# Two FFN tiles computed together, row block by row block, at the start of each FFN

## What is computed

```python
def swiglu(h, w1, w3, w2):
    return (jax.nn.silu(h @ w1) * (h @ w3)) @ w2
...
        yp = yp + swiglu(rmsnorm(yp, norm_ffn_g[l]), ffn_w1[l], ffn_w3[l], ffn_w2[l])
        ys = ys + swiglu(rmsnorm(ys, norm_ffn_g[l]), ffn_w1[l], ffn_w3[l], ffn_w2[l])
```

## Time and profile before

| | |
|---|---|
| time, median of 3 runs | 2050.66 us (2047.96 to 2051.35) |
| the profiled execution | 2048.34 us, span 2046.6 us |
| TensorE matmul (PE) busy | 1942.4 us, 95% |
| VectorE (DVE) busy | 742.4 us, 36% |
| ScalarE (ACT) busy | 450.3 us, 22% |
| mean granted TensorE clock | 0.965 of full |
| matmuls on `h_split` | 5184, 768.6 us busy |

### The profile page before, as it was taken

The page is one execution under the profiler, slowest core; times in us unless marked ns, Lnnn a source line. Parts: engine busy times, 40 slices in busy tenths (PEclk is TensorE's granted clock), DMA queues, the critical chain, the costliest instruction groups (busy, mean ns, idle before and its releaser), DMA issues.

```text
span 2046.6 us, 26656 instructions
## 1 busy us (share of the span) xinstructions
PE 1942.4 (95%) x11462; PEld 1622.3 (79%) x11462; DVE 742.4 (36%) x1203; ACT 450.3 (22%) x714; POOL 141.5 (7%) x149
## 2 busy tenths in 40 slices
PE   7999989899889999999998999799988999999998
PEld 5755556655659999999996999565565999999998
DVE  2099843312444332233334131631245333223222
ACT  3200231101422211111222114430133211121111
POOL 3001000000000000000004332200000000000000
PEclk9999986699999999999999999899999999999999
DMA  6322130150021112312120343411402211221120
GB/s 226 124 70 66 43 124 2 45 205 30 13 103 59 65 57 77 103 61 69 57 93 18 103 64 81 157 67 52 185 11 103 82 55 57 97 89 61 63 90 32
DMA packets 32036, 161.71 MB, mean 79 GB/s; under 512 B 8584, under 2 KB 9224, under 8 KB 18016
## 3 DMA queue, kind: packets, MB, share of 16 engines
q1 hardware_dynamic: 24032, 122.16, 18.1%
q0 software_dynamic: 7936, 38.60, 5.1%
HBM read 150.07 MB, written 10.42 MB: 78 GB/s over the span
## 4 chain that ended last, share of the span: by engine, by line
PE 92%; DVE 4%; ACT 2%; issue 1%; DMA 0%; POOL 0%; ACTq 0%; DVEq 0%
PE G L614 84%; PE Q L614 4%; PE S L614 3%; ACT rstd L1099 1%; DVE front L1417 1%; PE Q L1032 1%; DVE work L1721 1%; DVE h_split L1725 1%; ACT work L1099 0%; PE Q L884 0%; DVE stats L1836 0%; DMA front<-in_mem 0%; DVE front L1849 0%; DVE front L1619 0%; DVE stats L1659 0%
## 5 line engine op out<-in xcount | busy, mean ns | idle before, releaser
L614 PE MATMUL G<-h_split,w_split 128*128 128x320 f32 x5184 | 768.6, 310 | 10.6 <-DVE h_split L1725 10.5
L614 PEld LDWEIGHTS G<-h_split,w_split 128*128 128x128 f32 x5184 | 764.4, 189 | 12.8 <-issue 8.9
L614 PE MATMUL G<-front,ring 128*128 128x512 f32 (+2 forms) x1792 | 486.9, 434 | 12.4 <-DVE front L1417 7.0
L614 PEld LDWEIGHTS G<-front,ring 128*128 128x128 f32 x1792 | 279.5, 193 | 218.9 <-issue 212.6
L614 PE MATMUL G<-g_split,w_split 128*128 128x320 f32 x2112 | 310.4, 309 | 0.0
L614 PEld LDWEIGHTS G<-g_split,w_split 128*128 128x128 f32 x2112 | 309.9, 188 | 0.0
L1453 DVE TENSOR_TENSOR w_split<-ring,w_split 128x1024 fp32r<-128x1024 f32 (+2 forms) x152 | 164.4, 1083 | 359.3 <-ACT w_split L1099 359.3
L1099 ACT ACTIVATE w_split<-ring 128x1024 fp32r<-128x1024 f32 (+2 forms) x172 | 164.4, 957 | 517.8 <-PE G L614 517.8
L1503 DVE SCALAR_TENSOR_TENSOR front<-front,par 128x512 f32<-128x512 f32 x240 | 111.6, 546 | 0.1
L1099 ACT ACTIVATE work<-G 128x640 f32<-128x640 f32 x52 | 36.7, 706 | 331.9 <-PE G L614 331.9
L1737 DVE TENSOR_TENSOR work<-work,G 128x640 f32<-128x640 f32 x44 | 36.1, 821 | 183.9 <-PE G L614 183.9
(11 more groups left out here) (211 smaller groups left out, 1118.1 us busy)
## 6 DMA issues: line engine op xcount, KB each, us to landing
ring<-in_w_up0a SPq DMA_DIRECT2D x11, 1024.0 KB, 4.8
ring<-in_w_up0b SPq DMA_DIRECT2D x11, 1024.0 KB, 4.8
ring<-in_w_up1a SPq DMA_DIRECT2D x11, 1024.0 KB, 4.7
ring<-in_w_up1b SPq DMA_DIRECT2D x11, 1024.0 KB, 4.8
front<-in_mem_k POOLq DMA_DIRECT2D x8, 1024.0 KB, 11.7
front<-in_mem_v POOLq DMA_DIRECT2D x8, 1024.0 KB, 14.4
ring<-in_w_down0a SPq DMA_DIRECT2D x8, 704.0 KB, 4.1
ring<-in_w_down0b SPq DMA_DIRECT2D x8, 704.0 KB, 4.1
```

Source lines behind the costliest of these rows:

```text
L614: return nc.tensor.matmul(out, lhsT, rhs, start=start, stop=stop, **kw)
```

## The change

A new function `split_pair` computes tiles n and n + 1 together. For each row block k it waits once for the activations' low part, issues the 6 matmuls of tile n, and then the 6 of tile n + 1. The FFN's half "a" uses it for its first two tiles; half "b" and the loops are as before. Only TensorE's instructions are touched.

```diff
+            def split_pair(n, p, rhs, normed):
+
+
+                for j in range(2):
+                    begin(n + j)
+                pe.wait_ge(split, p + 2)
+                for k in range(KD):
+                    pe.wait_ge(applied, normed + k)
+                    for j in range(2):
+                        for wpart, xpart in ((0, 0), (0, 1), (1, 0)):
+                            w = ws[:, j, wpart, k * P:(k + 1) * P]
+                            for f in range(2):
+                                fr = slice(f * HT, (f + 1) * HT)
+                                m = mm(GF[(n + j) % 2][:, fr], w, rhs[:, xpart, k, fr],
+                                       k == 0 and wpart + xpart == 0, k == KD - 1 and wpart == 1)
+                        if k == KD - 1:
+                            m.then_inc(tile_done, 1)
+
...
-                    first = APPLIED[f"ffn{l}"] - KD + 1 if half == "a" else None
-                    for j in range(2):
-                        split_product(t0 + j, j, p0 + j, KD, hs, normed=first if j == 0 else None)
+                    if half == "a":
+                        split_pair(t0, p0, hs, APPLIED[f"ffn{l}"] - KD + 1)
+                    else:
+                        for j in range(2):
+                            split_product(t0 + j, j, p0 + j, KD, hs)
```

## The result

The changed kernel takes 2052.95 us (median of 20 runs, 2049.18 to 2055.51); the kernel before takes 2049.36 us (median of 20 runs, 2044.80 to 2051.35). The ratio is 1.0017, with a 95% interval from 1.0011 to 1.0023: slower by some 3.5 us, under the 0.2% that the prediction set as its bound. The prediction was 2053.0 us, with a range from 2049 to 2056.

A forecast was written before the change was run, and what follows sets the result against it. TensorE, busy 95% of the span, was taken as the bound. Row waits -3.9 and stalls +4.8 made +0.9 us; with one 1.5 us clock drop, +2.4 on the median 2050.66, stated as 2053.0 us, range 2049.0 to 2056.0.

The forecast's parts named there:

- all three sums: Whole kernel: +0.9 us with no clock drop behind the stalls, +2.4 with one, +3.9 with both.
- The end of the row waits: First two tiles of each FFN: all row waits but the first go, gaining 1.6 and 2.3 us, together 3.9.
- 3.5 us at half speed do 13: Second FFN's start: half speed lasts 3.5 us and covers 13 matmuls; the other 83 take 12.2 us.
- the two prices: TensorE's time per matmul: 0.147 us at full speed, about 0.267 us at half speed.
- The stall: Before each FFN's third tile: TensorE idles 2.3 us for split weights; 2.4 us per FFN with restart cost, 4.8 in all.
- the slow first matmul: Third tile's start, after the wait: 0.1 us added to each 2.3 us stall, as an estimate.
- The clock's price: Behind each stall: a half-speed stretch of 3.4 us costs 1.5 us, with two chances in three per stall.
- What lay behind it: Work queued after the stall: delay is taken once, fourth tile's weights are in time, loop stays at 7.04 us a tile.
- One sign was worded wrongly: Sign in the changed profile: ScalarE's first two reads of the FFN's tiles come 0.9 us apart in place of 7.04.
- The bank rule: Rival, first two tiles: alternating PSUM banks keeps all 96 matmuls at half speed; +20 us, 2071 us; chance 0.02.
- The stall stays small: Rival, before the third tile: the hidden chain is off the path, 3.9 us are kept, 2046.8 us; chance 0.06.
- The longer stretch of 6.8 us: Rival, third tile: half speed lasts 6.8 us, each stall costs 2.4 + 3.1 us; +7.1, 2057.8 us; chance 0.11.

The follow-up runs named there:

- the lag of five: Changed kernel with tile B five row blocks behind tile A (36 matmuls of B follow A's last): ratio 0.9975, again 0.9975 in the second run.
- the kernel with extra matmuls: Changed kernel with 14 extra matmuls, read by nobody, between the pair of tiles and the third tile: ratio 1.0002 against the kernel before.
- The lags: Changed kernel with tile B 1, 2, 3 or 5 row blocks behind tile A (changed kernel itself is 0): first ratios 0.9993, 0.9996, 0.9982, 0.9975.
- early weights and table: Changed kernel with the third tile's weights split early into a free buffer part and the SiLU table loaded ahead by a one-column SiLU: ratio 0.9986.
- the lag of three: Changed kernel with tile B three row blocks behind tile A (24 matmuls of B follow A's last): ratio 0.9982, then 0.9985 in the second run.
- the lag of one: Changed kernel with tile B one row block behind tile A (12 matmuls of B follow A's last): ratio 0.9993.
- the lag of two: Changed kernel with tile B two row blocks behind tile A (18 matmuls of B follow A's last): ratio 0.9996, then 0.9993 in the second run.
- the second experiment: Changed kernel with the third tile's weights split early into a free buffer part and each loop's first group written out, no early table load: ratio 0.9995.

## Why the prediction was right

**What was luck.** The prediction of 2053.0 us is 2.4 us on a base of 2050.66, the median of 3 runs. Measured were 3.6 us on a base of 2049.36, the median of 20. The two differences, 1.2 and 1.3 us, cancel, and so 2052.95 came out. The range held all three sums, with no half-speed stretch, one or two, so the time alone bears out none of them; the traces do.

**The end of the row waits.** Right in kind and size for the first FFN: the gate tile was read at 627.18, and the predicted end of the pair puts that at 627.85 - 0.88 + 0.2 = 627.17, so 1.6 us were gained. For the second FFN 2.3 us were predicted and 1.7 came. The term "3.5 us at half speed do 13" did not hold there: in the changed kernel the half level lasted to 1575.6 from a start at 1570.82, 4.8 us:

```profile
1570.80:1575.50 4.70, 4.68 (x18) 4.70 (x19) 4.70 (x7) 2.21 (x3) 0.00 (x0) 0.50 0.02 3
...
1575.00:1576.00 1.00, 1.00 (x7) 1.00 (x6) 1.00 (x3) 0.30 (x1) 0.00 (x0) 0.68 0.00 0
```

I had taken the length of that stretch from the one execution as if it belonged to the place. It is 3.0 to 6.1 us in the starts compared here (the shortest in the second FFN with the lag of five, the longest in that of the kernel with extra matmuls). Each microsecond of it takes some 0.45 us from the gain, worked out from the two prices: 1 - 0.147 / 0.267.

**The stall.** Predicted 2.3 us, or 2.4 with the slow first matmul; the trace shows 2.12 us of idling after the modelled end of the last matmul, and the third tile began at 630.14, where the sum gives 627.85 + 2.3 = 630.15. The lags are the proof that it is this chain: 2.12, 1.24, 0.36 us and nothing, with 6, 12, 18 and 24 matmuls to cover it, and nothing with early weights and table.

**The clock's price.** 1.5 us a stretch was predicted, and 1.52 measured with the extra matmuls. Wrong was the choice among the three sums: I took one drop as the middle (+2.4), and both stalls were followed by half speed, in both executions. With both, the prediction had +3.9; the FFN's starts of the trace give +4.5 (0.6 from the second FFN's smaller gain), and the runs +3.5, with an interval from 2.3 to 4.7.

**What lay behind it.** The product of gate and up tile and the next low part were in time, as predicted, and the loop kept 7.04 us a tile. One sign was worded wrongly: it is VectorE that reads the up tile, not ScalarE. What stood close together were ScalarE's two roundings of weights (from 627.78, 1.99 us for both), the second of which waits for the up tile.

**The bank rule.** The 96 matmuls over four PSUM banks ran as the sum at 0.267 and 0.147 us each says, in one stretch of 16.61 us, and with the cover restored nothing is lost. The Trainium skill's "TensorE: Matmul & The Clock Gate", section "A second HAM failure mode: psum-queue depth-cycling", names cycling through banks, by TensorE's short idles in it, as a cause of a swinging clock. The trace does not agree for this order of work: no idle is shown between the sixes, and the clock fell behind the wait for weights.

**The rivals.** "The stall stays small" is what the lag of three makes true: -3.1 us at the FFN's starts, where 3.9 were named. The longer stretch of 6.8 us behind the stall did not come: both lasted 3.4 us (630.2 to 633.6 and 1589.3 to 1592.7).

## What to carry to other kernels

When work is put together to remove small waits, look at what the spread of it used to hide: here the time between two tiles' ends was the cover of a chain of 3 us that reuses the first tile's buffer. The remedy is not to choose between the two orders but to set the lag between them: as much as the chain needs, and as little as the arriving rows allow. And cost an idle TensorE at its length and what its clock takes behind it, which here was 2.1 us and 1.5 us more, where 1.2 us of idling cost only itself. Whether the length of the idle time decides that is not shown: 2.2 us in the middle went both ways.

## What the runs showed of the hardware

A stall of 1.24 us was followed by full clock four times in four (the lag of one, and ScalarE's table load, in two FFNs each), and one of 2.12 us by half speed four times in four (two FFNs of the changed kernel, each in two executions, which came out alike and so are hardly more than two cases). One of 2.20 us went both ways: half speed in the kernel before, full speed with the lag of five. The same work in the middle of the program took 929.8 to 934.7 us, by where the half-speed stretches fell, and did so again in a second execution of the same kernel. A gain of 1 to 2 us in one place can therefore be more than doubled (the lag of five) or undone (the lag of two) in another that the change does not touch. In the second experiment ScalarE's table load stood behind the wait of the operation that needs it, and that left 1.25 us of idling of TensorE in each FFN, until a small SiLU was put ahead.
